# Queries and keys of a retention block: the rotation of 32-row groups by transfers instead of by a matrix product

## The reference, cut to what matters

```python
h = modulate(rms_norm(x, norm1_g[layer]), sh1, sc1)
q, k, v, g, ... = jnp.split(h @ w_in[layer] + b_in[layer], IN_SPLITS, axis=-1)   # q, k: 4 heads x 128

def rope_1d(x, ang):
    n_freq = ang.shape[-1]                       # 32
    x1, x2 = x[..., :n_freq], x[..., n_freq:]
    cos, sin = jnp.cos(ang), jnp.sin(ang)
    return jnp.concatenate([x1 * cos - x2 * sin, x1 * sin + x2 * cos], axis=-1)

def rope_grid(x, ang_row, ang_col):
    half = RET_QK_DIM // 2                       # 64
    return jnp.concatenate([rope_1d(x[..., :half], ang_row), rope_1d(x[..., half:], ang_col)], axis=-1)

q_h = rope_grid(split_heads(q, RET_HEADS).astype(f32), ang_row, ang_col)
k_h = rope_grid(split_heads(k, RET_HEADS).astype(f32), ang_row, ang_col) * k_scale
```

## Time and profile before

| | |
|---|---|
| time, median of 3 runs | 4257.39 us (4257.15 to 4257.42) |
| the profiled execution's own time | 4258.63 us |
| its span, from the first to the last instruction | 4256.8 us |
| mean granted TensorE clock over the span | 0.959 |
| TensorE busy over the span | 3793.8 us, 89% |
| the changed stage, from 519.5 to 656.2 | 136.7 us |
| TensorE busy in it | 125.96 us |
| ScalarE and VectorE busy in it | 10.99 and 30.65 us |

### The profile page before, as it was taken

One profiled execution on the slowest core, in us unless ns is written; L12 is line 12 of the kernel. 1 busy time (PEld: TensorE's weight loads), 2 busy tenths in 40 slices (PEclk: granted clock), 3 DMA queues, 4 the chain that ended last, 5 costly groups with the idle time before them and its releaser, 6 DMA issues. The chain is left out here.

```text
span 4256.8 us, 96995 instructions
## 1 busy us (share of the span) xinstructions
PE 3793.8 (89%) x42177; PEld 2439.0 (57%) x42177; DVE 1520.0 (36%) x2645; ACT 1015.0 (24%) x2384; POOL 604.8 (14%) x748
## 2 busy tenths in 40 slices
PE   7998899989999889999978998978888799996995
PEld 2443447874444478888854444447777644445774
DVE  5456225552112410000042666545555512222003
ACT  3200100040011122222243442034454211112333
POOL 1120000001100000000010001235555211000112
PEclk9999999999999889999989999989999999997998
DMA  8352311203112389999961001100000111206998
GB/s 293 131 163 79 121 59 60 79 12 70 42 34 93 121 310 393 394 390 395 398 219 25 9 3 45 40 6 5 4 4 4 64 48 52 98 37 226 384 388 317
DMA packets 242335, 597.53 MB, mean 140 GB/s; under 512 B 37097, under 2 KB 149640, under 8 KB 222123
## 3 DMA queue, kind: packets, MB, share of 16 engines
q1 hardware_dynamic: 200867, 471.27, 30.4%
q0 software_dynamic: 19120, 73.68, 5.0%
q10 hardware_dynamic: 22104, 49.00, 3.4%
HBM read 522.85 MB, written 71.05 MB: 140 GB/s over the span
## 5 line engine op out<-in xcount | busy, mean ns | idle before, releaser
L1790 PE MATMUL experts_bank<-experts_uT,ex_wu 128*64 128x96 f32 x9216 | 389.9, 247 | 25.9 <-PE experts_bank L1776 22.2
L1790 PEld LDWEIGHTS experts_bank<-experts_uT,ex_wu 128*64 128x64 f32 x9216 | 383.6, 137 | 42.7 <-issue 42.7
L1863 DVE TENSOR_TENSOR experts_hT<-experts_si,experts_bank 128x384 f32<-128x384 f32 (+1 forms) x68 | 31.3, 460 | 723.6 <-PE experts_bank L1790 723.6
L1790 PE MATMUL experts_bank<-experts_uT,b2z_hT 128*64 128x96 f32 x4096 | 179.1, 249 | 27.3 <-DMA b2z_hT<-in_w 14.8
L1790 PEld LDWEIGHTS experts_bank<-experts_uT,b2z_hT 128*64 128x64 f32 x4096 | 173.4, 139 | 42.2 <-issue 42.2
L1776 PE MATMUL experts_bank<-mixed_T,experts_hT 128*32 128x256 f32 (+1 forms) x2592 | 193.9, 451 | 0.0
L1776 PEld LDWEIGHTS experts_bank<-mixed_T,experts_hT 128*32 128x32 f32 x2592 | 110.4, 110 | 69.6
L1818 ACT ACTIVATE experts_uT<-experts_bank,all_modrun 128x96 f32<-128x96 f32 x296 | 99.3, 439 | 211.6 <-PE experts_bank L1771 211.6
L2413 POOL TENSOR_TENSOR b2z_hT<-b2z_hT,rwkv_level 128x256 f32<-128x256 f32 x192 | 140.2, 763 | 44.3 <-DVE b2z_hT L2892 33.5
L1399 DVE TENSOR_TENSOR merge_u<-merge_bank,merge_sg 128x512 f32<-128x512 f32 x16 | 11.1, 692 | 340.1 <-PE merge_bank L1332 340.1
L3294 PE MATMUL mh_sc<-mla_KTs,mh_QT 128*128 128x512 f32 x256 | 120.7, 594 | 5.9 <-ACT mla_KTs L3339 5.9
(11 more groups left out here) (618 smaller groups left out, 7264.0 us busy)
## 6 DMA issues: line engine op xcount, KB each, us to landing
ex_wu<-in_expert_w SPq DMA_DIRECT2D x72, 2048.0 KB
mixed_T<-in_expert_w SPq DMA_DIRECT2D x36, 2048.0 KB
b2z_hT<-in_w SPq DMA_DIRECT2D x64, 1024.0 KB
b2z_Z<-in_w SPq DMA_DIRECT2D x32, 1024.0 KB
keep_rows<-mix_hyT ACTq DMA_DIRECT2D x27, 768.0 KB, 8.7
keep_rows<-experts_yo ACTq DMA_DIRECT2D x68, 288.0 KB
mix_hT<-in_ada_w POOLq DMA_DIRECT2D x8, 2048.0 KB, 11.8
vg_w<-in_w_in SPq DMA_DIRECT2D x32, 512.0 KB, 4.5
```

What stands on the lines that cost most here:

```text
L1790: last = pe.matmul(bk[2 + j][c:c + 64, h * BT:(h + 1) * BT], wu[:, s, j, k, h * P + c:h * P + c + 64], uT[:, s, k, :], start=(k == 0), sto ...
```

## The change

The product with `rot` goes, and the matrix with it. Instead ScalarE, once it has copied a tile, issues four transfers inside SBUF: each takes 32 rows of the tile, 1024 float32 long, to the partner's 32 rows in `t`. The minus moves into the table of sines, which the host makes. VectorE then multiplies both products from SBUF, the second in one instruction and in place. The four banks that held turned tiles are not used any more.

The loops are written out. TensorE does not wait for its own results any longer; SP waits for `done` itself before it loads into a weight buffer. ScalarE issues a tile's transfers only when VectorE has finished the tile before (`roped`), since `t` is reused.

```diff
@@ phase_qk, sync
-            with sp.Fori(1, STEPS) as i:
-                for s in range(2):
-                    sp.wait_ge(wfree, i * 2 + (s + 1))
-                    sp.dma_start(wt[:, s, :, :], w[:, :, bass.ds(i * 256 + s * P, P)]).then_inc(wfull[s], 16)
+            for n in range(2, TILES):
+                sp.wait_ge(done, 2 * (n - 1))
+                sp.dma_start(wt[:, n % 2, :, :], w[:, :, n * P:(n + 1) * P]).then_inc(wfull[n % 2], 16)
@@ tensor
-            pe.sem_inc(wfree, 2)
-            pe.wait_ge(come, 32)
-            with pe.Fori(0, STEPS) as i:
...
-                    pe.wait_ge(done, i * 4 + (2 * s + 2))
-                    pe.sem_inc(wfree, 1)
-                for s in range(2):
-                    pe.wait_ge(roped, i * 2 + (s + 1))
-                    pe.wait_ge(evac, i * 4 + (2 * s + 6))
-                    for h in range(2):
-                        last = pe.matmul(bk[4 + 2 * s + h][:, :], rot, one(qk[:, bass.ds(i * 2 + s, 1), h * HALF:(h + 1) * HALF]), start=True, stop=True)
-                    last.then_inc(swapped, 1)
+            for n in range(TILES):
+                pe.wait_ge(wfull[n % 2], 16 * (n // 2) + 16)
+                if n >= 2:
+                    pe.wait_ge(evac, 2 * (n - 1))
+                for h in range(2):
+                    for k in range(KT):
+                        last = pe.matmul(bk[2 * (n % 2) + h][:, :], wt[:, n % 2, k, :], xT[:, k, hs[h]], start=(k == 0), stop=(k == KT - 1))
+                    last.then_inc(done, 1)
@@ scalar
+            for n in range(TILES):
+                for h in range(2):
+                    act.wait_ge(done, 2 * n + h + 1)
+                    act.activation(qk[:, n, hs[h]], bk[2 * (n % 2) + h][:, :], ACT.Identity, bias=K.cols[:, bcol + n:bcol + n + 1]).then_inc(evac, 1)
+                act.wait_ge(evac, 2 * n + 2)
+                if n:
+                    act.wait_ge(roped, n)
+                for q in range(4):
+                    here, there = 32 * q, 32 * (q ^ 1)
+                    act.dma_start(t[here:here + 32, 1, :], qk[there:there + 32, n, :]).then_inc(swapped, 16)
@@ vector
+            for n in range(TILES):
+                scale = sc[:, n // RH:n // RH + 1]
+                dve.wait_ge(evac, 2 * n + 2)
+                if n:
+                    dve.wait_ge(roped, n)
+                dve.scalar_tensor_tensor(t[:, 0, :], qk[:, n, :], scale, cs[:, 0, :], ALU.mult, ALU.mult).then_inc(turned, 1)
+                dve.wait_ge(swapped, 64 * (n + 1))
+                dve.scalar_tensor_tensor(t[:, 1, :], t[:, 1, :], scale, cs[:, 1, :], ALU.mult, ALU.mult).then_inc(turned, 1)
+                dve.wait_ge(turned, 2 * n + 2)
+                dve.tensor_tensor(qk[:, n, :], t[:, 0, :], t[:, 1, :], ALU.add).then_inc(roped, 1)
@@ constants
-    c["k_rope1"] = np.stack([np.cos(ang), np.sin(ang)], 1).astype(f)
...
-    c["k_rot1"] = rot.astype(f)
+    c["k_rope1"] = np.stack([np.cos(ang), sgn * np.sin(ang)], 1).astype(f)
```

## The result

The changed kernel takes 4231.9 us (median, 4228.41 to 4234.6) against 4257.27 for the kernel before (4253.63 to 4257.42) on the same chip: a ratio of 0.9944, 95% interval 0.993 to 0.9958. The profiled execution took 4232.74 us.

The account below looks back on a forecast made before the run. TensorE's instructions and pauses, then the chain from last projection to last addition, bound the stage. Its 17.8 us gain takes the profiled 4258.63 to 4240.8; the median, 1.24 lower, is 4239.6, range 4235 to 4249.

Parts of the forecast that it names:

- Start of the stage: TensorE's first matmul without loop setup and semaphore wait: 0.50 us after the copy instead of 0.80, gain 0.30.
- TensorE in one run: 256 projection matmuls without rotation matmuls or pauses: last weight load 15.2 us earlier, 109 us after the first.
- The loop: Per tile, copy, transfers and two VectorE instructions: 7.4 us, at the upper bound 12.9, hidden under TensorE's 13.7.
- B: Rival, chance 0.05: transfers at 4.4 us each, one after the other; loop of 20.6 us bounds the stage, 4301.
- C: Rival, chance 0.05: swap takes 11.5 to 13.5 us, loop bounds the stage, about no change, 4249 to 4266.
- The tail: After the last copy, swap of 4.7 us (bounds 3.6 and 10.2) plus 2.66 of VectorE; end at 637.98.
- rival A: Chance 0.10: each tile's four transfers land one after the other at 2.1 us; swap 8.7, gain 13.8, 4243.6.
- The stage: Whole edited stage: VectorE's last addition ends at 637.98 instead of 655.77, gain 17.8 us, bounds 18.9 and 12.3.
- After the stage: Next stage's weights and clock: costed at 0, bounds a gain of 1.1 and a loss of 2.7 us.
- The 1.1 us at the range's low end: Next stage's second 16 matmuls could start at 661.2 instead of 662.41; possible gain, added to the low end.
- T5: Experiments' theory: where TensorE's later code lies in 16 KB pieces sets the time behind the stage; input stage 183.6 or 181.

Follow-up runs that it names:

- e1: Changed kernel's straight code, but rotation still by TensorE products with the matrix, no transfers; 4244.93 us, ratio 0.9959 against the kernel before.
- e4: Changed kernel, but ScalarE waits for each of a tile's transfers before issuing the next; 4243.82 us, ratio 0.9954 against the kernel before.
- e12: Kernel before with 93 idle semaphore additions on TensorE's list, moving its later code, on chip 1; 4261.02 us, ratio 1.0008.
- e5: Kernel before with the stage's four loops written out and nothing else; 4251.9 us, ratio 0.9981.
- e15: Kernel before with the stage's loops written out and all else kept, run once more; 4252.63 us, ratio 0.9982.
- e10: Kernel before with 256 idle semaphore additions in TensorE's context stage, one whole 16 KB piece, on chip 2; 4275.15 us, ratio 1.0075.
- e11: Changed kernel with 163 idle semaphore additions in TensorE's context stage, on chip 2; 4244.04 us, ratio 0.9996 against the kernel before.
- e16: Changed kernel with 163 idle semaphore additions in three early places of TensorE's list, on chip 3; 4243.85 us, ratio 0.9982 against the kernel before.

## Why the prediction was wrong

The direction and the stage's mechanism were right; the time was not, by 7.7 us; 1.1 of them lie in the stage, the rest outside it.

- **Start of the stage**: forecast 0.50 after the last copy, measured 0.30 (521.10 to 521.40).
- **TensorE in one run**: forecast 109 us from first to last weight load, measured 630.49 - 521.37 = 109.1. Ten microseconds of matmuls and the pauses went as worked out; e1 shows that the pauses go without the transfers.
- **The loop**: one swap of 4.7 us stood for all tiles. Five tiles, with weights on the DMA engines, need 5.4 to 5.7, the sixth 9.8, the last two 4.4 and 4.2. With 2.5 of VectorE all lie under 13.7 per tile, so B and C did not happen.
- **The tail**: swap forecast 4.7 (bounds 3.6 to 10.2), measured 4.2. The fourth issue goes out 1.9 us after the copy and not 1.5, since an issue takes 0.61 us (the prediction put 0.4 from one to the next, where its own rival A reads 0.53), and lands 2.3 us later and not 3.2. Two sizes were off in opposite directions; that their sum came so near is in part luck. Rival A's serial landings appear only where e4 forces them.
- **The stage**: 18.9 from copy end to next stage, 17.8 forecast. Half a microsecond of the difference is the swap; the rest is 0.1 to 0.2 each at the start, the last copy, VectorE and the next stage's start. This error alone would have given 4238.5.
- **After the stage** is the step that failed: "they land up to 9.7 us after their issue, over 20 us ahead of need, so nothing is given back there", and "I cost it at 0, with bounds of a gain of 1.1 and a loss of 2.7". For the next stage that holds (198.6 us instead of 198.7). But I took the next stage for all that follows, and did not ask what removed loops and 349 more instructions do to code that is not edited. On chip 1 the time behind the stage is 3596.2 to 3598.3 in three traces of before, and 3582.8 to 3595.5 (mean 3589.5) in the eleven of every other kernel run there, e12 among them, which is before with its code moved, and e5, which is before without loops. The nearest of the eleven, e4, lies 0.7 us under the lowest of the three. It is not the transfers: outside the stage e1, which has none, gains 6.8 us by the medians, and e4, which has them, 6.4. About 5 us come with the loops written out alone (e5 and e15, medians) or with the code moved alone (e12, one trace); 2.5 of the latter are the late weights and the lower clock of the input stage, seen in its rows.

The 1.1 us at the range's low end was a bound on the next stage's start, where a span of 4256.8 us needed one for all the stages behind it; that made the range too narrow. The cause of what lies behind the stage stays open in the main: the other half of e12's 5.5 us (the chunk stage takes 558.6 to 566.6 in the traces on chip 1, so its 2.6 us rest on one trace), and the 2 to 5 us by which the changed kernel's medians gain more outside the stage (7 to 10) than e5's (5). That SP's issue is slow and the weights late when the packet falls there is seen five times out of five, and moving it away in e12 took the delay away; how it does so is not shown. On chips 2 and 3 the clock did not follow the delay, and e10, e11 and e16, which were to bring the long input stage back, did not, so that T5 rests on chip 1 alone.

## What to carry to other kernels

Price a moved instruction by its stage, and then give the stages behind it a margin of their own: here 0.1 to 0.2% came and went in stages that nobody edited, on one chip and not on another, so a gain under 10 us on such a span says little unless the edited stage shows it. Transfers inside SBUF for a rotation by 32 rows cost TensorE nothing, and here 4.2 us once, at the stage's end, if a tile's time covers one swap; there, split the last tile and its issues over two queues (2.4 us here).

## What was not expected of the hardware

- Four 128 KB transfers of 32 rows, SBUF to SBUF, on one queue take 4.2 us from the copy's end, 9.1 in a chain, 2.3 for one alone, and 5.4 to 9.8 beside weight loads. Each issue on ScalarE takes 0.61 us here, not the 0.34 to 0.36 of the earlier trace rows.
- An issue of SP into which a 16 KB instruction packet falls took 1.99 to 2.67 us, the same issue without one 1.20 to 1.64. A shift of TensorE's code by 93 instructions, which moves the packet away, went with 5.5 us less in 3597 on one chip.
- The same kernel before takes 4257 to 4259 us on chip 1, 4252 on chip 3 and 4243 on chip 2, with the edited stage at 136.3 to 136.5 us in every trace of it, those with additions included.
